# Mixer input projections by seven products of quarters, with the sums of weights formed on GpSimd and VectorE

## What is computed

```
h = rmsnorm(x, attn_norm[l])
proj = h @ w_in[l]                       # 1024 x 3088, split among four groups of heads
pa, pb, pc, pd = split(proj)             # A window attention, B gated linear, C stick breaking, D RWKV-7
x = x + concat(A(pa), B(pb), C(pc), D(pd)) @ w_out[l]
h = rmsnorm(x, ffn_norm[l])
x = x + swiglu(h) if l == 0 else x + top-2-of-8 experts(h)
```

## Time and profile before

| | us |
|---|---|
| median of 3 runs | 967.23 |
| lowest, highest | 963.81, 968.17 |
| the profiled execution | 964.62 |
| its span in the trace | 962.8 |
| PE busy | 942.8 |
| DVE, ACT, POOL busy | 380.4, 182.1, 134.8 |

### The profile page before, as it was taken

The page is one execution under the profiler, slowest core; times in us unless marked ns, Lnnn a source line. Parts: engine busy times, 40 slices in busy tenths (PEclk is TensorE's granted clock), DMA queues, the critical chain, the costliest instruction groups (busy, mean ns, idle before and its releaser), DMA issues.

```text
span 962.8 us, 28494 instructions
## 1 busy us (share of the span) xinstructions
PE 942.8 (98%) x12806; PEld 748.1 (78%) x12806; DVE 380.4 (40%) x799; ACT 182.1 (19%) x400; POOL 134.8 (14%) x154
## 2 busy tenths in 40 slices
PE   9999999899999999999999999899999999999996
PEld 7887875599999744788787559778778696969692
DVE  3415665676666555340566343022121213030204
ACT  3345241211011000224524221010000001010102
POOL 2000511123333322000052010000000000000000
PEclk9999999999999999999999999999999999999999
DMA  9843201445555545444310597989999999999931
GB/s 315 270 132 131 89 2 45 135 132 173 176 177 177 219 175 175 131 134 132 132 62 3 205 411 284 382 321 403 397 401 399 399 387 411 386 413 387 400 126 44
DMA packets 90114, 223.18 MB, mean 232 GB/s; under 512 B 6080, under 2 KB 53952, under 8 KB 89920
## 3 DMA queue, kind: packets, MB, share of 16 engines
q1 hardware_dynamic: 86528, 212.29, 59.2%
q0 software_dynamic: 1680, 5.90, 2.5%
q10 hardware_dynamic: 1840, 4.00, 1.2%
HBM read 215.89 MB, written 6.29 MB: 231 GB/s over the span
## 4 chain that ended last, share of the span: by engine, by line
PE 95%; ACT 2%; DVE 1%; issue 1%; POOL 0%; DVEq 0%; POOLq 0%; ACTq 0%
PE bank L629 93%; PE bank L640 1%; PE bank L1264 1%; ACT arena L1553 0%; PE bank L1008 0%; ACT hT L1408 0%; ACT arena L1550 0%; ACT arena L1413 0%; DVE tok L1813 0%; POOL small L1642 0%; PE bank L976 0%; DVE x_sb L1787 0%; DVE arena L2019 0%; ACT hT L1413 0%; PE bank L779 0%
## 5 line engine op out<-in xcount | busy, mean ns | idle before, releaser
L629 PE MATMUL bank<-arena 128*64 128x96 f32 (+6 forms) x8592 | 505.0, 276 | 4.9 <-issue 2.7
L629 PEld LDWEIGHTS bank<-arena 128*64 128x64 f32 (+4 forms) x8592 | 380.3, 136 | 128.1 <-issue 106.0
L629 PE MATMUL bank<-hT,arena 128*64 128x128 f32 (+2 forms) x1548 | 164.5, 307 | 1.5 <-ACT hT L1408 0.9
L629 PEld LDWEIGHTS bank<-hT,arena 128*64 128x64 f32 (+2 forms) x1548 | 145.5, 152 | 16.4 <-issue 4.4
L1787 DVE TENSOR_TENSOR arena<-arena 128x512 f32<-128x512 f32 (+3 forms) x135 | 122.7, 924 | 51.1 <-ACT arena L1413 26.3
L629 PE MATMUL bank<-arena,hT 128*128 128x256 f32 (+3 forms) x556 | 135.3, 405 | 1.6 <-ACT hT L1413 1.4
L629 PEld LDWEIGHTS bank<-arena,hT 128*128 128x128 f32 (+2 forms) x556 | 88.8, 181 | 38.3 <-issue 26.5
L1787 DVE TENSOR_TENSOR arena<-arena,bank 128x128 f32<-128x128 f32 (+3 forms) x135 | 49.2, 392 | 134.4 <-ACT arena L1616 106.1
L629 PE MATMUL bank<-tok,arena 128*64 128x128 f32 x1408 | 81.0, 273 | 0.0
L629 PEld LDWEIGHTS bank<-tok,arena 128*64 128x64 f32 x1408 | 78.2, 137 | 0.0
L1413 ACT COPY arena<-bank 128x512 f32<-128x512 f32 (+2 forms) x63 | 31.0, 496 | 172.8 <-PE bank L629 170.6
(11 more groups left out here) (203 smaller groups left out, 522.2 us busy)
## 6 DMA issues: line engine op xcount, KB each, us to landing
arena<-in_moe_w SPq DMA_DIRECT2D x128, 704.0 KB, 10.9
arena<-in_moe_w SPq DMA_DIRECT2D x40, 1024.0 KB, 8.6
arena<-in_ffn_w SPq DMA_DIRECT2D x33, 1024.0 KB, 5.3
arena<-in_w_in SPq DMA_DIRECT2D x22, 1024.0 KB, 5.2
arena<-in_w_out SPq DMA_DIRECT2D x8, 1024.0 KB, 4.9
arena<-in_moe_w SPq DMA_DIRECT2D x8, 512.0 KB, 12.2
arena<-in_w_in SPq DMA_DIRECT2D x2, 1088.0 KB, 5.4
consts<-in_consts SPq DMA_DIRECT2D x1, 1330.5 KB, 7.5
```

The costliest lines, as they stand in the source:

```text
L629: return nc.tensor.matmul(o, lhsT, rhs, start=start, stop=stop, skip_group_check=True)
```

## The change

Pieces P2 to P7 of layer 0 and P0 to P7 of layer 1 (`QUARTERED`, 14 pieces) go by seven products of quarters. With h11 to h22 the quarters of h (two halves of the features by two halves of the tokens) and w11 to w22 those of the piece, PE does, each product as 4 chunks times 2 halves of 128 x 64 by 128:

- `quarters_first`: w11 by h11 and w12 by h21 (quarters of `hT`, no sums);
- `quarters_third`: the sum s4 of weights by a quarter of `hT`; waits for `piece_summed`;
- `quarters_rest`: s2, s1, s3 and w22 by the four sums of h; waits for `h_summed`.

`project_quarters` does them in this order. In layer 1 P0 and P1 are interleaved: first P0, third P0, first P1, rest P0, third P1, rest P1. Each such piece has two banks, "a" (full after s2's product) and "b" (full at the end); even pieces use banks 0 and 1, odd ones 6 and 7, P7 banks 1 and 4.

The sums of h are formed by VectorE in each layer before P0 is mixed (`feature_sums`, four operations of 128 x 512). The sums of weights, s1 = w21 + w22 (written over w21 in the ring), s2 = s1 - w11, s3 = w11 - w21 and s4 = w12 - s2, each 128 x 512 and each waiting for the one before, are formed by GpSimd (`projection_piece_sums`); s3 of P4 to P7 in layer 0 and of P2 to P7 in layer 1 (`VECTOR_DIFFERENCES`) is formed by VectorE at the end of `quarters_out` of the piece two before, and GpSimd waits for it before it begins the other three. There are two sets of buffers, so the sums of a piece also wait until the piece two before is done. GpSimd forms P0's sums of layer 1 while the dense layer ends, and P1's when h is normalized.

ScalarE copies only the first quarter of a piece (`first_quarter`, 128 x 128). VectorE does the rest in `quarters_out`: two operations of 128 x 128 on bank a, then one of 128 x 256, one of 128 x 128 and one of 128 x 256 on bank b.

Besides: clearing `b_att` moves on GpSimd from after `al_mixed` of layer 0 to after P7 of each layer; the first `weight_difference` that ran beside the feed-forward's norm, number 1, now waits until the sums of h for the dense layer are formed; `WARM_UP_SHORT` goes from 35 products of 64 columns to 48 of 32.

The core of the diff:

```diff
+QUARTERED = [f"P{i}" for i in range(2, 8)], [f"P{i}" for i in range(8)]
+QUARTERED_ORDER = [(l, name) for l in range(DEPTH) for name in QUARTERED[l]]
+VECTOR_DIFFERENCES = [k for k in range(2, len(QUARTERED_ORDER)) if QUARTERED_ORDER[k - 2][0] == QUARTERED_ORDER[k][0]]
...
+            def quarter_product(o, weights, features, tokens, start=False):
+                for k in range(KC // 2):
+                    a, b = (features, weights) if tokens else (weights, features)
+                    last = mm_halves(o, a[:, k, :], b[:, k, :], start=(start and k == 0), stop=(k == KC // 2 - 1))
+                return last
...
+            def quarters_third(name, l, tokens=False):
+                k, _, _, _, s4 = projection_sums(name, l)
+                pe.wait_ge(sem("piece_summed"), k + 1)
+                wait_open(pe, f"{name}b", l)
+                at = 3 * P if tokens else 2 * P
+                quarter_product(bank(f"{name}b", l)[:, at:at + P], s4, hT[:, KC // 2:, P:SEQ], tokens, start=True)
...
-                project_features("P4", l, n0 + 4, both)
-                project_features("P5", l, n0 + 5, both)
-                project_tokens("P6", l, n0 + 6, GW)
-
-                wait_evacuated(pe, "P4", l)
-                wait_evacuated(pe, "P5", l)
+                project_quarters("P4", l)
+                project_quarters("P5", l)
+                project_quarters("P6", l, tokens=True)
+
+                pe.wait_ge(sem("c_q_ready"), l + 1)
+                wait_evacuated(pe, "P5b", l)
...
+            def projection_piece_sums(name, l):
+                k, s1, s2, s3, s4 = projection_sums(name, l)
+                wait_piece(pool, projection_piece(name, l))
+                if k >= 2:
+                    before, other = QUARTERED_ORDER[k - 2]
+                    wait_full(pool, f"{other}b", before)
+                w11, w12, w21, w22 = projection_quarters(name, l)
+                if k in VECTOR_DIFFERENCES:
+                    pool.wait_ge(sem("piece_subtracted"), VECTOR_DIFFERENCES.index(k) + 1)
+                else:
+                    link(g.tensor_tensor(s3, w11, w21, ALU.subtract))
+                link(g.tensor_tensor(s1, w21, w22, ALU.add))
+                link(g.tensor_tensor(s2, s1, w11, ALU.subtract))
+                g.tensor_tensor(s4, w12, s2, ALU.subtract).then_inc(sem("piece_summed"), 1)
...
+            def quarters_out(name, l, dst, step=P, tokens=False):
...
+                middle = pair_of(dst[:, P:P + 2 * step], P)
+                dve.wait_ge(sem("quarter_copied"), k + 1)
+                tt(dst[:, 0:P], first, a[:, P:2 * P], ALU.add)
+                frees(tt(first, first, a[:, 2 * P:3 * P], ALU.add), f"{name}a", l)
+                wait_evacuated(dve, f"{name}a", l)
+                wait_full(dve, f"{name}b", l)
+                link(tt(middle, pair_of(b[:, 0:2 * P], P), over(first, 2), ALU.add))
+                u3, p5 = (middle[:, 0, :], b[:, P:2 * P]) if tokens else (middle[:, 1, :], b[:, 0:P])
+                link(tt(dst[:, 2 * P + step:3 * P + step], u3, p5, ALU.add))
+                frees(tt(middle, middle, pair_of(b[:, 2 * P:4 * P], P), ALU.add), f"{name}b", l)
+                if k + 2 in VECTOR_DIFFERENCES:
+                    later, other = QUARTERED_ORDER[k + 2]
+                    wait_piece(dve, projection_piece(other, later))
+                    w11, _, w21, _ = projection_quarters(other, later)
+                    tt(projection_sums(other, later)[3], w11, w21, ALU.subtract).then_inc(sem("piece_subtracted"), 1)
...
                 if l == 0:
+                    pool.wait_ge(sem("h_summed"), 4 * H_SUMS[l, 1] + 4)
                     weight_difference(1)
...
                 last.then_inc(sem("rk_ready"), 1)
+                quarters_out("P4", l, c_e[0])
+                quarters_out("P5", l, region_f[:, 0:512])
+                quarters_out("P6", l, region_f[:, 512:1024], tokens=True)
```

More of the change, by code:

```diff
@@ L350, in build @@
         h_sums = tok[:, :, :].rearrange("p t d -> p (t d)").rearrange("p (s k t) -> p s k t", s=4, k=KC // 2)
+        first_piece = [extra[:, 1536 + P * b:1536 + P * b + P] for b in range(2)]
+        sum_parts = [[extra[:, 512 * i:512 * i + 512] for i in range(3)],
+                     [part("normed")[:, 0:512], part("normed")[:, 512:1024], part("b_att")]]
         def weight_sums(n):
@@ L692, in project_features, with quarters_first @@
                 fills(last, name, l)
+            def quarter_product(o, weights, features, tokens, start=False):
[3 more added lines that the diff above has]
+                return last
+            def quarters_first(name, l, features=None, tokens=False):
+                wait_piece(pe, projection_piece(name, l))
+                w11, w12, _, _ = projection_quarters(name, l)
+                wait_open(pe, f"{name}a", l)
+                a = bank(f"{name}a", l)
+                for i in (0, 1):
+                    if features:
+                        wait_evacuated(pe, features[i], l)
+                quarter_product(a[:, 0:P], w11, hT[:, 0:KC // 2, 0:P], tokens, start=True)
+                for i in (2, 3):
+                    if features:
+                        wait_evacuated(pe, features[i], l)
+                quarter_product(a[:, P:2 * P], w12, hT[:, KC // 2:, 0:P], tokens)
@@ L737, in layer_mixers @@
                 fills(last, "LA", l)
-                project_features("P3", l, n0 + 3, both)
+                project_quarters("P3", l)
                 wait_open(pe, "G", l)
@@ L1416, in both, with first_quarter @@
                 return ap.rearrange("p (c t) -> p c t", c=2)
+            def first_quarter(name, l):
+                k = QUARTERED_ORDER.index((l, name))
+                wait_full(act, f"{name}a", l)
+                if k >= 2:
+                    before, other = QUARTERED_ORDER[k - 2]
+                    wait_evacuated(act, f"{other}b", before)
+                nc.scalar.copy(first_piece[k % 2], bank(f"{name}a", l)[:, 0:P]).then_inc(sem("quarter_copied"), 1)
             def layer_mixers(l):
@@ L1424, in layer_mixers @@
                     nc.scalar.activation(trig[:, 2, :], trig[:, 2, :], ACT.Sin).then_inc(sem("sines"), 1)
-                evacuate("P0", l, raw[:, 6:8, 1:257], both(bank("P0", l)[:, :]))
-                evacuate("P1", l, raw[:, 0:2, 1:257], both(bank("P1", l)[:, :]))
+                for name, c0 in (("P0", 6), ("P1", 0)):
+                    if name in QUARTERED[l]:
+                        first_quarter(name, l)
+                    else:
+                        evacuate(name, l, raw[:, c0:c0 + 2, 1:257], both(bank(name, l)[:, :]))
                 act.wait_ge(sem("al_mixed"), l + 1)
@@ L1430, in layer_mixers @@
                 nc.scalar.activation(d_gl, mixed[:, 7, :], ACT.Sigmoid).then_inc(sem("gl_sig"), 1)
-                evacuate("P2", l, raw[:, 2:4, 1:257], both(bank("P2", l)[:, :]))
+                first_quarter("P2", l)
                 for name, off, dst in (("LW", "w0", d_lw), ("LA", "a0", d_a)):
@@ L1468, in layer_mixers @@
                 nc.scalar.activation(d_rn, d_rn, ACT.Sqrt).then_inc(sem("kk_roots"), 1)
-                evacuate("P7", l, b_raw, both(bank("P7", l)[:, :]))
+                first_quarter("P7", l)
                 evacuate("P8", l, b_v, both(bank("P8", l)[:, :]))
@@ L1703, in _ @@
             pool.wait_ge(sem("al_mixed"), 1)
-            g.memset(b_att[:, :, :, :], 0.0)
             g.memset(a_k[:, :, :], 0.0).then_inc(sem("cleared"), 1)
@@ L1709, in _ @@
                 if l:
+                    projection_piece_sums("P0", l)
                     row_powers()
+                    pool.wait_ge(sem("h_ready"), 2 * NT * (norm_index(l, 0) + 1))
+                    wait_evacuated(pool, "dn0", l - 1)
+                for name in QUARTERED[l][l:]:
+                    projection_piece_sums(name, l)
+                wait_full(pool, "P7b", l)
+                g.memset(b_att[:, :, :, :], 0.0).then_inc(sem("att_cleared"), 1)
                 for c in range(NT):
```

117 lines of the change are left out of this document (90 added, 27 removed), and 4 rows, old and new, of the table uses.

## The result

The changed kernel takes 972.39 us in the median of nine runs (970.62 to 979.67) against 963.94 for the kernel before beside it: 1.0097 times the time, 95% interval 1.0075 to 1.0118. I had forecast 966.0, which was 1.1 us less than a median of three, 967.23; set against the 963.94 beside it, my sum would have given 962.8, so it is off by 9.6 us and not by 6.4. The executions of the changed kernel form two groups, five of 970.6 to 972.4 and four of 978.3 to 979.7; the profiled one, 978.27 us with a span of 976.5, is of the upper group.

What follows compares the result with a forecast made beforehand. PE, busy 98% of the span, was taken as the bound. Saving 12.2, waits 12.5 and a removed wait of 1.4 summed to -1.1 us: 963.5 on the profiled execution, 966.0 as median, forecast 959 to 970, range widened to 956 to 971.

Steps and rivals of the forecast that it cites:

- The start: Shorter idle products before P0: P0 waits for h, not them; between 0.3 us gained and 0.5 lost, taken as 0.
- PE's saving of 12.2: Projections of both layers: each of 14 pieces falls from 6.98 to 6.11 us, saving 12.2 us.
- The walk of the waits: PE's waits for sums in the projections: 5.0 us in layer 0, 7.5 in layer 1, P6's 3.8 the largest.
- The turns of the two engines: POOL's sums and DVE's SBUF operations exclude each other: three sums cost DVE about 3.8 us, DVE's three operations cost POOL 1.7.
- The wait before the transposes: Ahead of the feed-forward's transposes: PE's wait for VectorE goes once sum number 1 is moved, 1.4 us gained.
- The clock, a rival: PE's clock may fall to 1.2 GHz in P6's wait: +2 to +9 us, 968 to 975; chance 0.15 with late DVE.
- The sign of being wrong that I had named: The clock row showing a digit below 9 near 60 or 450 us would prove the forecast wrong.
- a late VectorE: Rival: after the projections DVE's lateness outlives the logarithms, `ar` comes late, +1 to +2 us a layer; shares chance 0.15.

Runs made afterwards that it cites:

- the kernel of 956.42: Changed kernel with the old start, 13 idle products ahead of the router, and VectorE combining quarters of P3 to P6 earlier: 956.42 us, 0.9913 times the kernel before.
- the narrow sums: Changed kernel with the old start and loop in place, GpSimd forming 16 columns of every piece sum instead of 512: 953.64 us in one run.
- the next kernel of that order: Changed kernel with only the old start put back, 35 idle products of 64 columns: 1048.61 us, 1.0852 times the kernel before.
- the third: Changed kernel with the old start and 13 small idle products ahead of the router's product, restoring the loop's place: 969.04 us, 1.0041 times the kernel before.
- the second run: Kernel before with the change's start alone, 48 idle products of 32 columns for 35 of 64: 1015.08 us, 1.0514 times the kernel before.

## Why the prediction was wrong

- **The start: the step that failed first.** I wrote that P0 waits for h and not for the idle products, and took 0 between 0.3 gained and 0.5 lost. The trace that I had in hand spoke against it: the transposes follow the idle products without a gap (8.81 behind 1.09 + 7.79). P0 waits for whichever is later. Where the idle products end soonest, at 8.5 us, the transposes take 2.17 us for 1.96 and P0 begins at 11.02; where they end at 9.7, it begins at 12.08. Measured in the kernel before, the new start costs 1.4 us by the medians, and in 4 of 12 executions (4 of 9 of the changed kernel) 6 to 8 more; the profile of one of these shows PE at its lower level until 18 us. With the old start, the loop in place and all else the same, the changed kernel takes 969.04, inside my range. I also didn't ask why the number of products was changed. By my count it keeps the experts' loop in its place; that this was the reason is not on record.
- **PE's saving of 12.2: a term mis-sized.** The dense block's 6.11 is right for a piece between others of its kind, but P7, between products of other forms, takes 6.26 in the kernel of 956.42 (62.86 to 69.12) and took 6.91 before, not 6.98 (64.74 to 71.65):

```profile
62.86 2.84 PE L670 MATMUL bank<-hT,arena 128*64 128x128 f32 x48
65.53 3.66 PE L670 MATMUL bank<-tok,arena 128*64 128x128 f32 x64
69.12 14.08 PE L670 MATMUL bank<-arena,hT 128*128 128x256 f32 x64
```

```profile
64.74 7.07 PE L629 MATMUL bank<-hT,arena 128*128 128x256 f32 x32
71.65 13.98 PE L629 MATMUL bank<-arena,hT 128*128 128x256 f32 x64
```

  P3 to P6 of layer 0 took 6.11 to 6.26 without waits and 6.90 to 7.01 before, so both sides of my difference of 0.87 were a little off. Without any wait 14 pieces saved 6 x 0.68 + 8 x 0.73 = 9.9 us.
- **The walk of the waits held; its sizes were up to four times too large.** Layer 0: P5 0.92 for 1.2, P6 3.66 for 3.8, P2 none. Layer 1: sums of h 0.66 for 1.4, P2 0.43 for 0.7, P5 0.39 for 1.6, P6 3.66 for 3.8. Together 9.7 for 12.5, 7.3 of them P6's. The turns of the two engines, from which they were worked out, are shown by the rows of both and by the narrow sums: without GpSimd's work, none of the waits.
- **The wait before the transposes** went and was worth its 1.4: put back, it was there again with 1.42.
- **The clock, a rival with too small a chance.** In the changed kernel P6's wait brought the clock down in both layers, in the next kernel of that order in one, in the third again in both, for 1.6 to 2.7 us each, 4.3 us together in the changed kernel. With PE kept busy through the wait, and with the wait gone, it did not fall there; so the wait was the cause, though not one that works every time. The sign of being wrong that I had named, a digit below 9 in the clock row near 450 us, is there. My +2 to +9 had the size, my 0.15 (shared with a late VectorE) did not: I knew of no wait as long as this in the traces and let that speak for nothing happening, and so the sum held nothing for it.

The sum by measured terms: 9.7 of waits less 9.9 and 1.4 is -1.6; 4.3 of the clock at P6 and 1.4 of the start make +4.1. The lower group of the changed kernel stands 7.1 above the kernel before (971.07 for 963.94). Two falls in the RWKV stages at 1.4 would fill the gap; they stand in the profiled execution, which is of the upper group, and none stands in that of the kernel before. That profile also has 1.5 us less behind the router (388.2 for 389.7), which no run explains, so the sum closes only to within a microsecond or two. The upper group has 6 to 8 more from the start. With the old start in place 969.04 against 964.57 is left, +4.5: the waits, the saving and the clock at P6 make 2.7 of it, and one fall in the RWKV stage another 1.4.

So the idea was not at fault. The same products, sums and banks with VectorE's list in the order in which PE asks for its results, and the old start, run at 0.9913 of the kernel before.

## What to carry to other kernels

A program that loops over a body nearly as long as TensorE's instruction store depends on how many instructions stand ahead of it: when idle products, waits or products are added or removed, look at the number of instruction fetches and at "issue" waits before believing any comparison, and pad where the engine waits anyway. When work moves to a helper engine, write the list of the engine that feeds it in the order in which the helper needs its inputs. Put a price on the clock for a long wait on TensorE: here waits of 3.66 us cost themselves and in five of six cases 1.6 to 2.7 us more. Treat a changed constant in a diff as a step that needs a reason.

## What the hardware showed that I had not expected

- 13 idle products moved the experts' loop and cost 49 us in the kernel before (1015.08 for 966.54), 80 in the quartered one (1048.61 for 969.04); 64 and 63 more instruction fetches of 16.3 KB, about eight a pass. In the quartered kernel the clock fell beside them in every pass, which made about a quarter of the loss.
- The granted clock can be 1.00 in the record while transposes take 3.68 us for 1.96: the lower level at the program's start is not recorded.
- With start-up products of 32 columns, 4 of 12 and 4 of 9 executions (and none of 5 in the second run) took 6 to 8 us more; the one that was profiled had PE at the lower level until 18 us. With 64 columns this was seen in none of 23 runs of the kernel before and none of 12 of the changed one. Why, no run tells.
- GpSimd's additions of 16 columns took 0.22 us alone and up to 1.12 beside VectorE's scan, which itself took the same 1.23 as in the kernel before: here it is the short operation that pays for the turns.
